# Reordering the sixteen stick-breaking units of a two-block transformer kernel so that the widest unit of a head pair is worked one place later

## The chip, the cores and the metric

The kernel runs on one core of a Trainium2 chip. The metric is the device time of one execution in microseconds (us), lower being better. TensorE (PE in the profile; PEld is its weight load), VectorE (DVE), ScalarE (ACT) and GpSimd (POOL) each work through their own list of instructions in order and wait for each other by semaphores. SyncE (SP) issues most DMAs.

## The reference, cut to what matters

The model has three transformer layers on 512 tokens of width 1024. The first layer has two attentions side by side: eight heads of chunked attention ("a") and eight heads of stick-breaking attention ("b"). The change touches the second one only:

```python
def stick_breaking_attention(q, k, v):
    ...
    for blk in range(s // SB_BLOCK):
        q_start = blk * SB_BLOCK
        k_end = q_start + SB_BLOCK
        logits = jnp.einsum("bqhd,bkhd->bhqk", q[:, q_start:k_end],
                            k[:, :k_end]).astype(jnp.float32) * scale
        strict = (q_start + jnp.arange(SB_BLOCK))[:, None] > jnp.arange(k_end)[None, :]
        log_beta = jax.nn.log_sigmoid(logits)
        log_keep = jnp.where(strict, jax.nn.log_sigmoid(-logits), 0.0)
        log_tail = lax.cumsum(log_keep, axis=3, reverse=True) - log_keep
        weights = jnp.where(strict, jnp.exp(log_beta + log_tail), 0.0).astype(v.dtype)
        outs.append(jnp.einsum("bhqk,bkhd->bqhd", weights, v[:, :k_end]))
```

Afterwards both attention outputs are normalized (their mean squares over the features), scaled by gains, joined and multiplied by `w_out`.

## The kernel before

The kernel holds activations with features on the 128 partitions and the 512 tokens along the free dimension. Each large product is made from a high and a low part of both operands, three matrix products for one. The engine programs are written out by hand, each in its own order, with counting semaphores between them.

Eight heads are four **pairs** `p`, and each pair has four **units** `r` of one block of 128 keys each. Unit `r` treats key block `3 - r` against the queries from that block on, so it is `r + 1` blocks of 128 wide; with two heads its tiles are 256, 512, 768 and 1024 elements wide per partition. I call these widths one to four. `sb_unit(u)` (L705) gives pair, row and first query of the unit at place `u` of the order. Before, it is `u // 4, u % 4`, so the widths run 1 2 3 4, 1 2 3 4, 1 2 3 4, 1 2 3 4.

A unit passes these steps:

1. `sb_qk` (L977, matmuls L985 and the mask L988) on PE: scores into one of three pairs of PSUM banks.
2. The clip (L2323) on DVE: the minimum of the scores and 40, into one of two buffers `tmp`.
3. `softplus` (L1510, instructions L1513 and L1515) on ACT: Exp, then Ln, in place.
4. `sb_larger` (L2278, L2287) on DVE: the maximum of scores and softplus, into `sb_pl`, a ring of three.
5. `sb_tail_sum` (L992) on PE: L998 with the triangle for the unit's own block, and L1005 with ones for what lies in the newer key blocks. For `r = 1` L1005 reads the width-one unit's `sb_pl` directly, for `r` of 2 and 3 it reads the sums `sb_sum`, which `sb_add` (L2290, L2302 and L2303 on DVE) makes after `r = 1` and `r = 2`.
6. `sb_weigh` (L1660, L1667) on ACT: Exp of the banks, which gives the weights `sb_w`.
7. `sb_values` (L1009, L1020) on PE, once for each pair after its width-four unit; `sb_save` (L1670) on ACT copies the result out.

The engines run this as a hand-made pipeline. At step `u` DVE does `sb_larger(u - 1)`, the clip of `u`, then `sb_add(u - 1)` if there is one, and then whatever else was placed there. ACT does `sb_weigh(u - 2)`, then Exp and Ln of `u`. PE does `sb_tail_sum(u)`, the values of the last pair when its turn comes, and `sb_qk(u + 2)`:

```python
                sb_tail_sum(u)
...
                if u and u % 4 == 0:
                    sb_values(u // 4 - 1)
                if u + 2 < SB_UNITS:
                    sb_qk(u + 2)
```

Other work sits at fixed steps: half of a memory product at PE's step 1; the first norm's root on ACT at step 8 (`root("oa")`, two activation table loads and a square root) with its reciprocals on DVE at steps 8 to 10 (L2336); its scaling `scale_a` (L2307) and low parts `low_a` (L2312) on DVE at steps 12 and 13; the high parts `high` on ACT at step 12; squares of the saved pairs at 8, 12 and 16. Before PE's step 15 stand six matmuls of `w_out`. After step 15 follow the rest of them, the values of pair 3, the second norm and the `w_out` phase, which waits for it.

Of the kernel before, what the change touches and what calls it, by code (L numbers as in the profile page):

```python
# [15 lines left out]
ALU = mybir.AluOpType  # L16
# [3 lines left out]
P = 128  # L20
SEQ = 512
# [79 lines left out]
def program(nc, a, out):  # L101
    ctx = ExitStack()
    with ctx:
# [16 lines left out]
        act_lo = at("act_lo", [P, KT, SEQ], o_act + 16 * KB, FP32R)  # L120

        sb_pl = at("sb_pl", [P, 3, 2, SEQ], o_act)
        sb_w = at("sb_w", [P, 2, 2, 1280], o_act + 12 * KB)
        sb_sum = at("sb_sum", [P, 2, 2, SEQ], o_m + 80 * KB)
        p_low_0 = at("p_low_0", [P, 2, 768], o_m + 64 * KB)
# [576 lines left out]

        SB_UNITS = 4 * 4

        def sb_unit(u):  # L705

            p, r = u // 4, u % 4
            return p, r, P * (3 - r)

        def sb_banks(u):  # L710

# [39 lines left out]
        def _(pe):  # L751
# [240 lines left out]
            def sb_tail_sum(u):  # L992

                p, r, q0 = sb_unit(u)
                b = [bank[sb_banks(u) + h] for h in range(2)]
                pe.wait_ge(sb_plus, u + 1)
                for h in range(2):
                    last = pe.matmul(b[h][:, q0:SEQ], neg_upper[:, :], sb_pl[:, u % 3, h, q0:SEQ],  # L998
                                     start=False, stop=True, skip_group_check=True)
                if r >= 2:  # L1000
                    pe.wait_ge(sb_added, 2 * p + r - 1)
                if r:
                    for h in range(2):
                        older = sb_pl[:, (u - 1) % 3, h, :] if r == 1 else sb_sum[:, r % 2, h, :]
                        last = pe.matmul(b[h][:, q0 + P:SEQ], neg_ones[:, :], older[:, q0 + P:SEQ],  # L1005
                                         start=False, stop=True, skip_group_check=True)
                last.then_inc(sb_tail, 1)

            def sb_values(p):  # L1009
                if p == 0:  # L1010
                    pe.wait_ge(out_saved, PAIR0["mem_a"])
                if p == 1:
                    pe.wait_ge(root_ready, NORM["oa"] + 1)
                if p >= 2:
                    pe.wait_ge(sb_saved, p - 1)
                pe.wait_ge(sb_weights, 4 * p + 4)
                for kj in range(4):
                    for h in range(2):
                        head = 2 * p + h
                        last = pe.matmul(bank[p % 2][HD * h:HD * h + HD, P * kj:SEQ],  # L1020
                                         v_tok[1][:, kj, HD * head:HD * (head + 1)],
                                         sb_weight(p, 3 - kj, h), start=kj == 0, stop=True,
                                         skip_group_check=True)
                last.then_inc(sb_out, 1)
# [136 lines left out]
            for u in range(SB_UNITS):  # L1161
                if u == 15:
                    pe.wait_ge(w_ready, C0["w_out"] + 1)
                    pe.wait_ge(act_ready, SPLIT0["w_out"] + 4)
                    pe.wait_ge(sb_saved, 3)
                    part(C0["w_out"], 0, 0, range(2), o_0, start=True)
                sb_tail_sum(u)
                if u == 1:
                    pe.wait_ge(out_saved, 4)
                    mem_half(1, 1)  # L1170
                if u == 4:
                    pe.wait_ge(mem_saved, 2)
                if u and u % 4 == 0:
                    sb_values(u // 4 - 1)
                if u + 2 < SB_UNITS:
                    sb_qk(u + 2)
                if u == 5:
                    norm_sum("oa")
            part(C0["w_out"], 0, 0, range(2, 4), o_0)
            sb_values(3)  # L1180
# [223 lines left out]
        def _(act):  # L1404
# [273 lines left out]
            for u in range(SB_UNITS + 2):  # L1678
                if u >= 2:
                    sb_weigh(u - 2)  # L1680
                if u < SB_UNITS:
                    softplus(sb_clip(u), sb_clamped, sb_exped, sb_logged, u + 1)
                if u == 0:
                    square("oa", 3, o_raw[0][:, 3, :], (out_saved, 4))
                if u in (5, 9, 13):
                    sb_save(u // 4 - 1)
                if u == 8:
                    root("oa")
                    act.preload_act_table_set("natural_log_exp_and_others")
                if u in (8, 12, 16):  # L1690
                    square_b(u // 4 - 2)
                if u == 12:
                    for t in range(4):
                        high("w_out", t, o_hi_0[0][:, t, :], buf=rel[0])
            sb_save(3)
# [132 lines left out]
        def _(dve):  # L1828
# [449 lines left out]
            def sb_larger(u):  # L2278

                p, r, q0 = sb_unit(u)  # L2280
                b = sb_banks(u)
                dve.wait_ge(sb_logged, u + 1)
                if u == 0:
                    dve.wait_ge(chunk_done, C0["w_out"])
                if u >= 3:
                    dve.wait_ge(sb_tail, u - 1 if r == 3 else u - 2)
                dve.tensor_tensor(sb_pl[:, u % 3, :, q0:SEQ], banks[:, b:b + 2, q0:SEQ], sb_clip(u), ALU.max)\  # L2287
                    .then_inc(sb_plus, 1)

            def sb_add(u):  # L2290

                p, r, q0 = sb_unit(u)
                dve.wait_ge(sb_plus, u + 1)
                if u == 1:
                    dve.wait_ge(out_saved, PAIR0["mem_a"])
                if r == 1:
                    older = sb_pl[:, (u - 1) % 3, :, q0 + P:SEQ]
                else:
                    dve.wait_ge(sb_added, 2 * p + 1)
                    older = sb_sum[:, 0, :, q0 + P:SEQ]  # L2300
                new, dst = sb_pl[:, u % 3, :, :], sb_sum[:, (r + 1) % 2, :, :]
                dve.tensor_copy(dst[:, :, q0:q0 + P], new[:, :, q0:q0 + P])  # L2302
                dve.tensor_tensor(dst[:, :, q0 + P:SEQ], new[:, :, q0 + P:SEQ], older, ALU.add)\  # L2303
                    .then_inc(sb_added, 1)
# [10 lines left out]
            for u in range(SB_UNITS + 1):  # L2315
                if u:
                    sb_larger(u - 1)
                if u < SB_UNITS:
                    if u == 0:
# [2 lines left out]
                    b = sb_banks(u)  # L2322
                    dve.tensor_scalar(sb_clip(u), banks[:, b:b + 2, sb_unit(u)[2]:SEQ], CLAMP, None,  # L2323
                                      ALU.min).then_inc(sb_clamped, 1)
                if u and (u - 1) % 4 in (1, 2):
                    sb_add(u - 1)
                if u == 3:
                    mem_group(1)
                if u == 1:
                    add_squares("oa", 3)  # L2330
                if u in (13, 16):
                    add_squares("ob", 1 + u // 16)
                for n in {8: (0, 1), 9: (2,), 10: (3,)}.get(u, ()):
                    c = P * n
                    dve.wait_ge(root_ready, NORM["oa"] + 1)
                    part = dve.reciprocal(rms[:, c:c + P], rms[:, c:c + P])  # L2336
                    if n == 3:
                        part.then_inc(rms_ready, 1)
                if u == 12:
                    dve.wait_ge(rms_ready, NORM["oa"] + 1)  # L2340
                    for t in range(4):
                        scale_a(t)
                    low_a(0)
                    low_a(1)
                if u == 13:
                    low_a(2)
                    low_a(3)
            add_squares("ob", 3)
# [248 lines left out]
```

## Time and profile before

| | |
|---|---|
| median of 3 runs | 1846.5 us (1846.32 to 1847.78) |
| profiled execution, its own time | 1844.83 us |
| span of the profiled execution | 1843.1 us |
| mean granted TensorE clock | 0.995 |
| PE busy | 1793.1 us (97%), 8628 matmuls |
| DVE busy | 1080.7 us (59%) |
| ACT busy | 723.1 us (39%) |

The span runs from the first to the last instruction; the execution's time is 1.7 us more. Busy time is the union of an engine's instructions, so 97% of PE's span says that it seldom stood still, not that it ran at its peak. The stick-breaking units take from about 227 to 302 us of the span.

### The profile page before, as it was taken

How to read it: one execution, taken by the hardware profiler on the slowest of the kernel's cores; microseconds unless marked ns; L12 is line 12 of the kernel's file. 1: busy time of each engine (PE TensorE's matmuls, PEld its weight loads, DVE VectorE, ACT ScalarE, POOL GpSimd, SP SyncE). 2: the span in 40 equal slices, each digit the busy share in tenths (PEclk: the TensorE clock that was granted, in tenths of full speed). 3: DMA queues.
4: the chain of work that ended last, by engine and by line, in shares of the span. 5: the costliest groups of instructions: out<-in, count | busy, mean ns of one | idle time of the engine just before them, and what ended most of it. 6: DMA issues, size and time to landing. Idle time of an engine off the chain costs nothing.

```text
span 1843.1 us, 23045 instructions
## 1 busy us (share of the span) xinstructions
PE 1793.1 (97%) x8628; PEld 1445.4 (78%) x8628; DVE 1080.7 (59%) x1569; ACT 723.1 (39%) x1015; POOL 38.8 (2%) x78
## 2 busy tenths in 40 slices
PE   6999988999999999999999999999999999999998
PEld 5787645788888888878888888889766788888886
DVE  6576755656655425765767675245467467776423
ACT  4212654343443323443443433233356344444322
POOL 3110000000000000000000000000000000000000
PEclk9999999999999999999999999999999999999999
DMA  9685110423322233322322322323401223322231
GB/s 328 236 320 179 47 52 19 141 80 101 104 91 91 87 102 93 107 70 71 112 91 91 105 100 80 108 81 105 164 24 47 69 92 95 110 91 91 91 103 69
DMA packets 148059, 195.32 MB, mean 106 GB/s; under 512 B 3646, under 2 KB 133000, under 8 KB 144284
## 3 DMA queue, kind: packets, MB, share of 16 engines
q1 hardware_dynamic: 141272, 155.28, 25.9%
q0 software_dynamic: 6576, 39.13, 5.6%
q8 instruction: 43, 0.70, 0.2%
q14 instruction: 20, 0.16, 0.0%
q10 hardware_dynamic: 148, 0.05, 0.0%
HBM read 189.15 MB, written 5.29 MB: 105 GB/s over the span
## 4 chain that ended last, share of the span: by engine, by line
PE 89%; DVE 5%; ACT 3%; DMA 1%; issue 1%; SPq 0%; DVEq 0%; ACTq 0%
PE bank L770 21%; PE bank L771 21%; PE bank L772 21%; PE bank L833 3%; PE bank L835 2%; PE bank L834 2%; PE bank L1385 2%; PE bank L1383 2%; PE bank L1384 2%; PE bank L916 2%; PE bank L952 2%; PE bank L933 1%; PE bank L813 1%; PE bank L814 1%; PE bank L815 1%
## 5 line engine op out<-in xcount | busy, mean ns | idle before, releaser
L1832 DVE TENSOR_TENSOR w_lo<-w_stage,w_hi 128x2048 fp32r<-128x2048 f32 (+2 forms) x137 | 301.3, 2199 | 469.5 <-ACT w_hi L1410 469.3
L770 PE MATMUL bank<-act_hi,w_hi 128*128 128x512 f32 x1232 | 482.9, 392 | 4.8 <-DVE act_lo L2163 3.4
L771 PE MATMUL bank<-act_lo,w_hi 128*128 128x512 f32 x1232 | 480.1, 390 | 0.0
L772 PE MATMUL bank<-act_hi,w_lo 128*128 128x512 f32 x1232 | 480.0, 390 | 0.0
L1410 ACT ACTIVATE w_hi<-w_stage 128x2048 fp32r<-128x2048 f32 (+3 forms) x139 | 255.5, 1838 | 490.5 <-PE bank L772 370.1
L770 PEld LDWEIGHTS bank<-act_hi,w_hi 128*128 128x128 f32 x1232 | 231.7, 188 | 57.4 <-issue 3.3
L772 PEld LDWEIGHTS bank<-act_hi,w_lo 128*128 128x128 f32 x1232 | 231.7, 188 | 48.4
L771 PEld LDWEIGHTS bank<-act_lo,w_hi 128*128 128x128 f32 x1232 | 231.7, 188 | 47.8 <-issue 0.5
L770 PE MATMUL bank<-mid_hi,w_hi 128*128 128x512 f32 x352 | 136.9, 389 | 0.0
L771 PE MATMUL bank<-mid_lo,w_hi 128*128 128x512 f32 x352 | 136.9, 389 | 0.0
L772 PE MATMUL bank<-mid_hi,w_lo 128*128 128x512 f32 x352 | 136.9, 389 | 0.0
L1553 ACT ACTIVATE mid_hi<-tmp 128x512 f32 x66 | 40.7, 633 | 97.1 <-DVE tmp L2036 97.1
L772 PEld LDWEIGHTS bank<-mid_hi,w_lo 128*128 128x128 f32 x352 | 66.1, 188 | 13.8
L770 PEld LDWEIGHTS bank<-mid_hi,w_hi 128*128 128x128 f32 x352 | 66.1, 188 | 13.7
L771 PEld LDWEIGHTS bank<-mid_lo,w_hi 128*128 128x128 f32 x352 | 66.1, 188 | 13.6
L1383 PE MATMUL bank<-w_hi,mid_hi 128*128 128x512 f32 x176 | 68.8, 391 | 0.0
L1385 PE MATMUL bank<-w_lo,mid_hi 128*128 128x512 f32 x176 | 68.5, 389 | 0.0
L1384 PE MATMUL bank<-w_hi,mid_lo 128*128 128x512 f32 x176 | 68.5, 389 | 0.0
L1545 ACT ACTIVATE tmp<-tmp,vec 128x512 f32<-128x512 f32 x44 | 33.5, 809 | 70.0 <-DVE tmp L1850 70.0
L1545 ACT ACTIVATE mid_val<-tmp,vec 128x512 f32 x44 | 33.5, 808 | 69.8 <-DVE tmp L1850 69.8
L1850 DVE SCALAR_TENSOR_TENSOR tmp<-bank,rms 128x512 f32<-128x512 f32 x88 | 56.4, 682 | 0.0
L1982 DVE SCALAR_TENSOR_TENSOR ada_acc<-ada_stage,stats,ada_acc 128x2048 f32<-128x2048 f32 x21 | 48.8, 2347 | 1.5 <-DMA ada_stage<-in_w_ada 1.1
(396 smaller groups left out, 2594.8 us busy)
## 6 DMA issues: line engine op xcount, KB each, us to landing
ada_stage<-in_w_ada POOLq DMA_DIRECT2D x24, 1024.0 KB, 7.8
w_stage<-in_w_up SPq DMA_DIRECT2D x22, 1024.0 KB, 5.0
w_stage<-in_a_ffn_in SPq DMA_DIRECT2D x22, 1024.0 KB, 5.1
w_stage<-in_b_ffn_in SPq DMA_DIRECT2D x22, 1024.0 KB, 5.1
w_stage<-in_w_in SPq DMA_DIRECT2D x12, 1024.0 KB, 5.2
w_stage<-in_b_ffn_out SPq DMA_DIRECT2D x10, 1024.0 KB, 5.1
w_stage<-in_w_down SPq DMA_DIRECT2D x8, 1024.0 KB, 5.0
w_stage<-in_a_ffn_out SPq DMA_DIRECT2D x8, 1024.0 KB, 5.0
```

Source lines behind the costliest of these rows:

```text
L770: pe.matmul(dst, wh, mh, start=start and k == 0, stop=False)
L771: pe.matmul(dst, wh, ml, start=False, stop=False)
L772: last = pe.matmul(dst, wl, mh, start=False, stop=stop and k == nk - 1)
L833: pe.matmul(dst, wh, mh, start=start and k == ks[0], stop=False)
L1383: pe.matmul(dst, mh, hi[:, k, :], start=j == 0 and k == 0, stop=False)
L1384: pe.matmul(dst, ml, hi[:, k, :], start=False, stop=False)
L1385: last = pe.matmul(dst, mh, lo[:, k, :], start=False, stop=j == 5 and k == nk - 1)
L1410: act.activation(w_hi[slot][:, 0:n], w_stage[slot][:, 0:n], ACT.Copy).then_inc(w_hi_done, 1)
L1545: act.activation(conv_tile(f, i, s, m), conv_src(f, s, m)[:, :], ACT.Identity, scale=w2, bias=b).then_inc(tap_started, 1)
L1832: dve.tensor_tensor(w_lo[slot][:, 0:n], w_stage[slot][:, 0:n], w_hi[slot][:, 0:n].bitcast(FP32), ALU.subtract).then_inc(w_ready, 1)
L1850: return dve.scalar_tensor_tensor(out=dst, in0=src[:, :], scalar=scale, in1=norm[:, :], op0=ALU.mult, op1=ALU.mult)
L1982: dve.scalar_tensor_tensor(out=acc, in0=ada_stage[n][:, :], scalar=k, in1=acc, op0=ALU.mult, op1=ALU.add).then_inc(ada_added, 1)
```

## The change

The order of the units is written out in a list. The width-four unit of pairs 0, 1 and 2 changes places with the width-one unit of the next pair, so that the widths run 1 2 3 1 4 2 3 1 4 2 3 1 4 2 3 4. What hangs on places follows: the values of a pair, its save, the first norm's sum and root, the reciprocals, the scaling and the low and high parts come one step later. The width-one unit's softplus gets a buffer of its own, `sb_pl_first`, because its reader (`r = 1`) is now two places behind it. Two waits are added on DVE: `sb_larger` of a width-four unit waits for its pair's second sum, and the second `sb_add` of a later pair waits until the last width-four tail sum has read `sb_sum`. The wait of `sb_larger` on `sb_tail` for width four goes from `u - 1` to `u - 2`. No instruction that computes is added or removed, and no DMA is touched.

```diff
+        sb_pl_first = at("sb_pl_first", [P, 2, SEQ], o_m + 18 * KB)
...
+        SB_ORDER = [(0, 0), (0, 1), (0, 2), (1, 0), (0, 3), (1, 1), (1, 2), (2, 0), (1, 3), (2, 1), (2, 2), (3, 0),
+                    (2, 3), (3, 1), (3, 2), (3, 3)]
+
         def sb_unit(u):
 
-            p, r = u // 4, u % 4
+            p, r = SB_ORDER[u]
             return p, r, P * (3 - r)
+
+        def sb_at(p, r):
+
+            return SB_ORDER.index((p, r))
+
+        def sb_plus_of(u):
+
+            return sb_pl_first[:, :, :] if sb_unit(u)[1] == 0 else sb_pl[:, u % 3, :, :]
...
 # sb_tail_sum
-                    last = pe.matmul(b[h][:, q0:SEQ], neg_upper[:, :], sb_pl[:, u % 3, h, q0:SEQ],
+                    last = pe.matmul(b[h][:, q0:SEQ], neg_upper[:, :], sb_plus_of(u)[:, h, q0:SEQ],
...
-                        older = sb_pl[:, (u - 1) % 3, h, :] if r == 1 else sb_sum[:, r % 2, h, :]
+                        older = sb_pl_first[:, h, :] if r == 1 else sb_sum[:, r % 2, h, :]
...
 # sb_values
-                pe.wait_ge(sb_weights, 4 * p + 4)
+                pe.wait_ge(sb_weights, sb_at(p, 3) + 1)
...
 # PE's loop
-                if u == 4:
+                if u == 5:
                     pe.wait_ge(mem_saved, 2)
-                if u and u % 4 == 0:
+                if u in (5, 9, 13):
                     sb_values(u // 4 - 1)
                 if u + 2 < SB_UNITS:
                     sb_qk(u + 2)
-                if u == 5:
+                if u == 6:
                     norm_sum("oa")
...
 # ACT's loop
-                if u in (5, 9, 13):
+                if u in (6, 10, 14):
                     sb_save(u // 4 - 1)
-                if u == 8:
+                if u == 9:
                     root("oa")
                     act.preload_act_table_set("natural_log_exp_and_others")
-                if u in (8, 12, 16):
+                if u in (9, 13, 16):
                     square_b(u // 4 - 2)
-                if u == 12:
+                if u == 13:
                     for t in range(4):
                         high("w_out", t, o_hi_0[0][:, t, :], buf=rel[0])
...
 # sb_larger
-                    dve.wait_ge(sb_tail, u - 1 if r == 3 else u - 2)
-                dve.tensor_tensor(sb_pl[:, u % 3, :, q0:SEQ], banks[:, b:b + 2, q0:SEQ], sb_clip(u), ALU.max)\
+                    dve.wait_ge(sb_tail, u - 2)
+                if r == 3:
+                    dve.wait_ge(sb_added, 2 * p + 2)
+                dve.tensor_tensor(sb_plus_of(u)[:, :, q0:SEQ], banks[:, b:b + 2, q0:SEQ], sb_clip(u), ALU.max)\
                     .then_inc(sb_plus, 1)
...
 # sb_add
                 if r == 1:
-                    older = sb_pl[:, (u - 1) % 3, :, q0 + P:SEQ]
+                    older = sb_pl_first[:, :, q0 + P:SEQ]
                 else:
                     dve.wait_ge(sb_added, 2 * p + 1)
+                    if p:
+                        dve.wait_ge(sb_tail, sb_at(p - 1, 3) + 1)
                     older = sb_sum[:, 0, :, q0 + P:SEQ]
...
 # DVE's loop
-                if u and (u - 1) % 4 in (1, 2):
+                if u and sb_unit(u - 1)[1] in (1, 2):
                     sb_add(u - 1)
...
-                if u in (13, 16):
+                if u in (14, 16):
                     add_squares("ob", 1 + u // 16)
-                for n in {8: (0, 1), 9: (2,), 10: (3,)}.get(u, ()):
+                for n in {9: (0, 1), 10: (2,), 11: (3,)}.get(u, ()):
...
-                if u == 12:
+                if u == 13:
                     dve.wait_ge(rms_ready, NORM["oa"] + 1)
                     for t in range(4):
                         scale_a(t)
                     low_a(0)
                     low_a(1)
-                if u == 13:
+                if u == 14:
                     low_a(2)
                     low_a(3)
```

## Rows read from the trace of the kernel before

**Rows 1.** The page's chain of waits, shares of the span by engine.

```profile
PE 89%; DVE 5%; ACT 3%; DMA 1%; issue 1%; SPq 0%; DVEq 0%; ACTq 0%
```

**Rows 2.** One window, a pair long: stretch, length, busy times, granted clock, DMA.

```profile
262.50:280.50 18.00, 13.97 (x68) 7.56 (x68) 11.02 (x17) 12.63 (x17) 0.00 (x0) 1.00 0.00 0
```

**Rows 3.** Waits between 226 and 302 us: total, times, longest.

```profile
DVE tmp L2323 <- PE bank L988: 11.0, 5, 4.2
```

**Rows 4.** Timeline of DVE: start, duration, instruction, idle time before it.

```profile
239.92 1.22 DVE L2323 TENSOR_SCALAR tmp<-bank 128x1024 f32<-128x1024 f32 x1 [2.79 <-PE bank L988]
...
244.49 0.41 DVE L2323 TENSOR_SCALAR tmp<-bank 128x256 f32<-128x256 f32 x1
...
245.84 0.42 DVE L2287 TENSOR_TENSOR sb_pl<-bank,tmp 128x256 f32<-128x256 f32 x1 [0.93 <-ACT tmp L1515]
...
250.49 0.69 DVE L2323 TENSOR_SCALAR tmp<-bank 128x512 f32<-128x512 f32 x1 [4.23 <-PE bank L988]
...
252.54 0.69 DVE L2287 TENSOR_TENSOR sb_pl<-bank,tmp 128x512 f32<-128x512 f32 x1 [1.36 <-ACT tmp L1515]
...
289.28 0.96 DVE L2323 TENSOR_SCALAR tmp<-bank 128x768 f32<-128x768 f32 x1 [1.17 <-PE bank L988]
...
292.03 0.96 DVE L2287 TENSOR_TENSOR sb_pl<-bank,tmp 128x768 f32<-128x768 f32 x1 [1.25 <-ACT tmp L1515]
292.90 1.21 DVE L2323 TENSOR_SCALAR tmp<-bank 128x1024 f32<-128x1024 f32 x1
...
296.33 1.22 DVE L2287 TENSOR_TENSOR sb_pl<-bank,tmp 128x1024 f32<-128x1024 f32 x1 [1.42 <-ACT tmp L1515]
```

**Rows 5.** Timeline of PE in pair 3, at the full clock.

```profile
280.65 1.98 PE L998 MATMUL bank<-sb_pl,neg_upper 128*128 128x512 f32 x4 [1.51 <-DVE sb_pl L2287]
...
283.85 0.70 PE L985 MATMUL bank<-qkv 64*128 64x256 f32 x4
...
285.17 0.71 PE L998 MATMUL bank<-sb_pl,neg_upper 128*128 128x128 f32 x4 [0.40 <-DVE sb_pl L2287]
285.81 2.37 PE L1020 MATMUL bank<-sb_w,vb_tok 128*64 128x512 f32 x16
288.11 0.92 PE L985 MATMUL bank<-qkv 64*128 64x384 f32 x4
...
289.08 1.08 PE L998 MATMUL bank<-sb_pl,neg_upper 128*128 128x256 f32 x4
...
290.54 1.13 PE L985 MATMUL bank<-qkv 64*128 64x512 f32 x4
...
293.04 1.56 PE L998 MATMUL bank<-sb_pl,neg_upper 128*128 128x384 f32 x4 [1.15 <-DVE sb_pl L2287]
```

**Rows 6.** Timeline of PE in pair 0, from where the orders part.

```profile
238.53 1.13 PE L985 MATMUL bank<-qkv 64*128 64x512 f32 x4
...
239.72 1.51 PE L998 MATMUL bank<-sb_pl,neg_upper 128*128 128x384 f32 x4
...
242.02 0.49 PE L985 MATMUL bank<-qkv 64*128 64x128 f32 x4
...
244.63 3.26 PE L998 MATMUL bank<-sb_pl,neg_upper 128*128 128x512 f32 x4 [1.91 <-DVE sb_pl L2287]
...
249.53 0.70 PE L985 MATMUL bank<-qkv 64*128 64x256 f32 x4
```

**Rows 7.** One window of the slow stretch, columns as in Rows 2.

```profile
246.00:247.00 1.00, 1.00 (x3) 0.48 (x2) 0.26 (x1) 0.00 (x0) 0.00 (x0) 0.50 0.42 168
```

**Rows 8.** Timeline of DVE: the first norm's extra work.

```profile
265.89 1.76 DVE L2336 RECIPROCAL rms<-rms 128x128 f32<-128x128 f32 x2 [2.93 <-ACT rms L1440]
267.57 0.36 DVE L2287 TENSOR_TENSOR sb_pl<-bank,tmp 128x256 f32<-128x256 f32 x1
...
280.84 2.73 DVE L2307 SCALAR_TENSOR_TENSOR rel<-oa_raw,vec,rms 128x512 f32<-128x512 f32 x4
...
284.69 0.42 DVE L2287 TENSOR_TENSOR sb_pl<-bank,tmp 128x256 f32<-128x256 f32 x1
```

More of the change, by code:

```diff
@@ L2296, in sb_add @@
                 if r == 1:
-                    older = sb_pl[:, (u - 1) % 3, :, q0 + P:SEQ]
+                    older = sb_pl_first[:, :, q0 + P:SEQ]
                 else:
                     dve.wait_ge(sb_added, 2 * p + 1)
+                    if p:
+                        dve.wait_ge(sb_tail, sb_at(p - 1, 3) + 1)
                     older = sb_sum[:, 0, :, q0 + P:SEQ]
-                new, dst = sb_pl[:, u % 3, :, :], sb_sum[:, (r + 1) % 2, :, :]
+                new, dst = sb_plus_of(u), sb_sum[:, (r + 1) % 2, :, :]
                 dve.tensor_copy(dst[:, :, q0:q0 + P], new[:, :, q0:q0 + P])
```

## The prediction, made before the changed kernel was run

> **What bounds the kernel now.** I read four views. The chain of waits first: PE carries 89% of it, DVE and ACT together 8% [rows 1], so nearly all of the kernel is a row of matmuls and a gain can only lie where PE is not the chain. The unit stage is such a place. In the window of one pair, PE is busy 13.97 of 18.00 us and DVE and ACT no more, 11.02 and 12.63 [rows 2]: no engine is full, the chain crosses from one to the other. The waits say where: the clip waits five times for the scores, 11.0 us in all [rows 3]. The timeline then gives each step its price, and I lay out the new order with them.
>
> **The prices.** DVE and ACT form one loop: clip, Exp, Ln, larger, and the next clip starts 0.08 us before the larger ends. From a clip to its larger it takes 1.35, 2.05, 2.75 and 3.43 us for widths one to four, and from there to the next clip the larger's own 0.42, 0.69, 0.96 or 1.22 less 0.08 [rows 4]. So the loop alone needs 1.69, 2.66, 3.63 and 4.57 us a unit, 12.5 for four.
>
> PE starts a tail sum 0.06 us after its larger ends: 0.48 after its start for width one (284.69 to 285.17), 1.01 for three (292.03 to 293.04), so 0.75 and 1.28 for two and four [rows 4, 5, 8]. A tail sum holds PE 0.64, 1.46, 2.30 and 3.20 us (285.17 to 285.81, 289.08 to 290.54, 239.72 to 242.02, 280.65 to 283.85), values 2.30, and scores 0.97 for width three and 1.19 for four, that is 0.21 less a width, so 0.76 and 0.56 for two and one [rows 5, 6]. A clip can start 0.2 us after the scores have let PE go: 1.39 after their start for width four (238.53 to 239.92), 1.17 for three, 0.96 for two, hence 0.74 for one [rows 4, 5, 6]. PE's work for four units comes to 7.60 + 3.48 + 2.30 = 13.4 us.
>
> The hole lies here: the scores of unit u + 2 stand behind the tail of u. Before, the width-four tail (1.28 + 3.20) and the scores behind it take 5.4 us from the larger to the clip, while the loop beside it has a width-one unit, 2.8 us.
>
> **The change, part by part.** It adds and removes no computing instruction and no DMA; SP's and POOL's queues are passed by nothing. What moves is the order. Laid out from 238.53, where both orders part (times of the new order, PE at its full clock; the row's 238.53 stands, since the matmuls of the memory half before it stay) [rows 6]:
>
> *Places 3 to 7.* Scores 3 (width one) start at 238.53, tail 2 at 239.09, scores 4 (width four) at 241.39, so clip 4 starts at 242.78 and larger 4 at 246.21. Tail 3 and scores 5 are over at 243.93; PE then has nothing until tail 4 at 247.49. That is an idle stretch of 3.56 us where before it was 1.91 [rows 6]. Tail 4 ends at 250.69, and scores 6 open clip 6 at 251.86, where DVE was free at 250.00. Larger 6 starts at 254.61. Tail 5, the values of pair 0 and scores 7 follow each other on PE from 251.66 to 255.98; clip 7 starts at 256.16, tail 6 at 255.98, scores 8 at 258.28, clip 8 at 259.67.
>
> *Places 8 to 11.* Larger 8 is at 263.10, clip 9 at 264.24, tail 8 from 264.38 to 267.58. ACT's root now comes after Ln of unit 9. Before, the reciprocals waited 2.93 us after the clip had ended [rows 8], and of this Exp and Ln of width one were 0.9, so the root costs 2.03. Ln 9 ends at 266.25, the reciprocals start at 268.28, hold DVE 1.68 (265.89 to 267.57) [rows 8], and larger 9 starts at 269.96 instead of 266.29. The stall of 3.7 us is the one that was there before, with another unit under it. Clip 10 follows at 270.56, larger 10 at 273.31; tail 9, the values and scores 11 keep PE from 270.70 to 275.02, tail 10 to 277.32, so clip 11 is at 275.20 and clip 12, behind scores 12, at 278.71. The other two reciprocals lie beside Exp and Ln; the norm's sum lies in PE's idle time before tail 8 (2.7 us); without that cover it would put its 0.9 us on the loop.
>
> *Places 12 to 15.* Larger 12 is at 282.14, tail 12 from 283.42 to 286.62, clip 13 at 283.28. Scaling and two low parts took DVE from 280.84 to 284.69, 3.85 us [rows 8]; now they run from 283.88, and larger 13 comes at 287.73 instead of 285.33. Tail 13 starts at 288.47, then values 2, then scores 15 at 292.23: clip 15 at 293.62, larger 15 at 297.05. Before, larger 15 started at 296.33 [rows 4]. The other low parts and the squares delay larger 14 by about 0.5 us, under clip 15's wait for PE. The added waits, on sums and tails which are over by then, cost nothing: what stands behind them on DVE, the larger of width four and the second add, has its input later than they are met. If such a wait were met late, DVE's clip and then ACT's Exp would be late by as much. The saves and weights on ACT come out at least 0.5 us before PE asks for them.
>
> So at the full clock the new order is **0.7 us slower** than the row. The same hole stands twice in a pair now, each smaller: the wide scores wait behind the width-three tail with a width-one unit as cover (clips 4, 8 and 12), and those of width three behind the wide tail (clip 6; at clip 10 the root hides it). In exchange, before, pair 0 had lost more than the pattern.
>
> **The clock.** In 246 to 247 us the granted clock is 0.50, 1.2 GHz, after PE had stood idle for 1.91 us [rows 6, 7]. The wide tail then takes 4.90 us (244.63 to 249.53) instead of 3.20, a loss of 1.7, and clip 5 waits 4.23 [rows 4, 6]. That loss is in the row of 296.33. In the new order PE idles for 3.56 us in the same place, before the same wide tail. I take it that the clock falls again: 1.7 us more, and nothing hides it, since clip 6 waits for that tail. The sum is 0.72 + 1.70 = **2.4 us**. The idle stretches before tails 8 and 12, 2.7 and 3.6 us, may bring it too, but there tail 9 waits for the root (2.1 us of room) and tail 13 for the scaling (0.9 us of room), so at most 0.8 us would come through. The bounds of the clock's part are thus 0 and 2.5 us.
>
> The Trainium skill (TensorE: Matmul & The Clock Gate, Part 1, "What's actually happening") says that the array falls to half its clock when it has been idle and comes back after sustained work, and that the point shifts from run to run. By that rule all three long idle stretches would be followed by half clock, which by the rooms above would make 3.2 us instead of 2.4. The trace agrees on the two levels, 1.00 and 0.50.
>
> After larger 15 both orders do the same, and the `w_out` phase waits for the second norm, so the shift stays to the end. The profiled execution took 1844.83 us and would take 1847.2; the median of the runs shown lies 1.7 above the profiled one, and I carry the shift to it: 1846.5 + 2.4 = **1848.9 us**.
>
> **The rivals.** *No fall of the clock* (0.22): 0.7 us more, 1847.2. For it: the tails at 280.65 and 293.04 follow idle times of 1.5 and 1.15 us with no sign of it [rows 5]; against it: the new stretch is twice the one that brought it. *A faster kernel* (0.08): PE turns the wide tails and scores out early enough that the clips don't wait for them. It decides if the waits of clips 4, 6, 7, 8, 11, 12 and 15 for PE, in my layout 1.4, 1.9, 0.7, 1.8, 1.0, 1.1 and 1.2 us, all but vanish, 9.1 us together; half of them gone gives 0.7 - 4.6, 1842.6. Against it stand PE's prices, which are read at the full clock. *Clock at half after every long idle stretch, without the rooms* (0.15): 0.7 + 3 x 1.7 = 5.8 us more, 1852.3. It decides when the slow stretch reaches values and scores as well as the tail. The likeliest case has 0.55.
>
> **How the numbers follow.** A measurement of this kernel tells about 0.2%, 3.7 us, from no change. The likeliest case and the first rival lie within it, 0.77, less a little for prices that I carried over 13 places with perhaps 0.1 us of error each: 0.76 within, 0.16 slower, 0.08 faster. The range runs from 1845.0 (first rival less 2.2) to 1851.8 (towards the last rival) and leaves out the faster one.
>
> **What would show it right or wrong.** In the profile after, PE should be idle for about 3.6 us before the first wide tail (L998, 512 columns, about 247.5) and the clock at 0.5 behind it; clip 15 near 295.3 and larger 15 near 298.7 us; the reciprocals' stall of about 3.7 us before larger 9. The prediction is wrong if the clips' waits for PE go well under 11 us in total, or if a fall of the clock lasts beyond one tail.

## The result and the profile after

The changed kernel took 1849.84 us (median of 13 runs, 1848.39 to 1853.91) and the kernel before 1847.68 us (13 runs, 1846.23 to 1850.22). The ratio is 1.0018, with a 95% interval of 1.0011 to 1.0025: some 3.3 us slower, between 2.0 and 4.6; the two medians lie 2.2 us apart. The forecast shift was 2.4 us. The forecast time was 1848.9, 0.9 below the measured one, which lies in the range (1845.0 to 1851.8); the median of before had been taken as 1846.5, from three runs.

The profiled execution took 1849.67 us, span 1848.0, which is 4.9 more than the span before. To find where they came in, I take two marks: the first clip, and the start of the larger of place 15. From here on "clip 11", "larger 11" and "tail 11" are the starts of these steps for the unit at place 11 of the order, and the "stage" runs from clip 0 to larger 15. VectorE's timeline after:

```profile
228.82 0.42 DVE L2339 TENSOR_SCALAR tmp<-bank 128x256 f32<-128x256 f32 x1
...
244.59 1.23 DVE L2339 TENSOR_SCALAR tmp<-bank 128x1024 f32<-128x1024 f32 x1 [1.26 <-PE bank L1000]
248.03 1.22 DVE L2301 TENSOR_TENSOR sb_pl<-bank,tmp 128x1024 f32<-128x1024 f32 x1 [2.21 <-ACT tmp L1527]
...
255.31 0.96 DVE L2339 TENSOR_SCALAR tmp<-bank 128x768 f32<-128x768 f32 x1 [3.41 <-PE bank L1000]
...
267.68 0.68 DVE L2339 TENSOR_SCALAR tmp<-bank 128x512 f32<-128x512 f32 x1
271.71 1.76 DVE L2352 RECIPROCAL rms<-rms 128x128 f32<-128x128 f32 x2 [3.36 <-ACT rms L1452]
273.39 0.63 DVE L2301 TENSOR_TENSOR sb_pl<-bank,tmp 128x512 f32<-128x512 f32 x1
...
287.29 2.73 DVE L2323 SCALAR_TENSOR_TENSOR rel<-oa_raw,vec,rms 128x512 f32<-128x512 f32 x4
289.94 1.29 DVE L2328 TENSOR_TENSOR o_lo<-rel,o_hi 128x512 fp32r<-128x512 f32 x2
291.14 0.69 DVE L2301 TENSOR_TENSOR sb_pl<-bank,tmp 128x512 f32<-128x512 f32 x1
...
301.23 1.22 DVE L2301 TENSOR_TENSOR sb_pl<-bank,tmp 128x1024 f32<-128x1024 f32 x1 [1.42 <-ACT tmp L1527]
```

The larger of place 15 starts at 301.23 against 296.33 [rows 4], 4.9 later; so all of the span's difference is there by then, and the work behind it takes the same time in both. The first clip starts at 228.82. In the trace of before it starts at 227.00:

```profile
227.00 0.42 DVE L2323 TENSOR_SCALAR tmp<-bank 128x256 f32<-128x256 f32 x1
```

So 1.82 us lie ahead of the stage, among instructions that the change does not touch, and **3.08 us in the stage**: 72.41 us from the first clip to that larger, against 69.33. The part ahead varies by itself: in the fourteen profiles of this study the first clip starts between 227.00 and 230.25. In this execution TensorE ran below its full clock there (0.66 over 210 to 220 us, second window below; 1.00 in the trace of before).

TensorE's timeline after, around the first and the last of the three wide tails that moved:

```profile
244.99 0.70 PE L997 MATMUL bank<-qkv 64*128 64x256 f32 x4
245.62 0.29 PE L1000 MATMUL bank<-strict_neg,ident_b 128*128 128x128 bf16 x2
249.31 3.61 PE L1010 MATMUL bank<-sb_pl,neg_upper 128*128 128x512 f32 x4 [3.40 <-DVE sb_pl L2301]
252.75 1.46 PE L1017 MATMUL bank<-sb_sum,neg_ones 128*128 128x384 f32 x4
254.13 0.92 PE L997 MATMUL bank<-qkv 64*128 64x384 f32 x4
...
267.81 1.98 PE L1010 MATMUL bank<-sb_pl,neg_upper 128*128 128x512 f32 x4 [2.54 <-DVE sb_pl L2301]
...
286.83 3.62 PE L1010 MATMUL bank<-sb_pl,neg_upper 128*128 128x512 f32 x4 [3.40 <-DVE sb_pl L2301]
290.28 1.45 PE L1017 MATMUL bank<-sb_sum,neg_ones 128*128 128x384 f32 x4
291.67 0.92 PE L997 MATMUL bank<-qkv 64*128 64x384 f32 x4
```

Windows after (columns as in [rows 2]), and the waits between 226 and 305 us:

```profile
210.00:220.00 10.00, 8.71 (x50) 5.20 (x50) 8.33 (x32) 6.39 (x20) 0.00 (x0) 0.66 0.20 66
250.00:251.00 1.00, 1.00 (x2) 0.34 (x1) 0.00 (x0) 0.97 (x2) 0.00 (x0) 0.50 0.00 0
288.00:289.00 1.00, 1.00 (x3) 0.48 (x2) 1.00 (x3) 0.97 (x3) 0.00 (x0) 0.50 0.00 0
```

```profile
PE bank L1010 <- DVE sb_pl L2301: 13.2, 6, 3.4
DVE tmp L2339 <- PE bank L1000: 13.1, 9, 3.4
```

TensorE stands idle for 3.40, 2.54 and 3.40 us before the three wide tails, where it was 1.91 before the first of them in the old order [rows 6]. The clock is at half behind the first and the third, and each of these tails takes 4.8 us instead of 3.2 (249.31 to 254.13, 286.83 to 291.67), while the second has 1.98 for its 512 columns as at full clock. The clips wait for scores nine times, 13.1 us, where it was five times and 11.0 [rows 3].

### The profile page after: what moved, and what is told of

It is laid out like the page before. It is cut to its first block, busy times and chain, and to the rows that moved or that the text cites. A ratio compares the mean times of both kernels' runs of the same rounds, so it can differ in the third digit from the quotient of the medians.

```text
span 1848.0 us, 23045 instructions
## 1 busy us (share of the span) xinstructions
PE 1797.4 (97%) x8628; PEld 1448.9 (78%) x8628; DVE 1080.9 (58%) x1569; ACT 723.8 (39%) x1015; POOL 38.9 (2%) x78
## 4 chain that ended last, share of the span: by engine, by line
PE 90%; DVE 4%; ACT 3%; DMA 2%; issue 1%; POOL 0%; DVEq 0%; ACTq 0%
PE bank L782 21%; PE bank L783 21%; PE bank L784 20%; PE bank L845 3%; PE bank L847 2%; PE bank L846 2%; PE bank L1397 2%; PE bank L1395 2%; PE bank L1396 2%; PE bank L928 2%; PE bank L964 2%; PE bank L945 1%; PE bank L825 1%; PE bank L826 1%; PE bank L827 1%; DMA ada_stage<-in_w_ada 1%
## 5 line engine op out<-in xcount | busy, mean ns | idle before, releaser
L1395 PE MATMUL bank<-w_hi,mid_hi 128*128 128x512 f32 x176 | 68.9, 392 | 0.0
```

The source lines that it names most:

```text
L1395: pe.matmul(dst, mh, hi[:, k, :], start=j == 0 and k == 0, stop=False)
```

## The experiments

The runs of one kernel differ by up to 0.4% here (1844.3 to 1851.2 us in 29 runs of before), so each kernel is read twice: by its ratio to the kernel before, and by the stage, which the trace of one execution gives to 0.1 us. "Falls" counts the stretches at half clock inside the stage in that execution. "Layout" is the stage as laid out by hand at full clock, in the prediction or in the expectation of the run.

| kernel | ratio (95%) | stage | falls | layout |
|---|---|---|---|---|
| before | | 69.33 | 1 | |
| changed | 1.0018 (1.0011 to 1.0025) | 72.41 | 2 | 70.05 |
| old order in new code | 0.9993 (0.9984 to 1.0002) | 67.62 | 0 | |
| before, filled | 0.9995 (0.9986 to 1.0004) | 67.63 | 0 | |
| changed, three fills | 1.0011 (1.0002 to 1.0020) | 71.70 | 1 | 70.05 |
| changed, four fills | 1.0010 (1.0001 to 1.0020) | 70.09 | 0 | 70.05 |
| first exchange alone | 1.0013 (1.0004 to 1.0022) | 69.63 | 1 | 68.15 |
| middle exchange alone | 1.0014 (1.0004 to 1.0023) | 70.32 | 1, long | 69.6 |
| last exchange alone | 1.0014 (1.0005 to 1.0023) | 73.68 | 3 | 69.4 |
| changed, scaling at step 12 | 1.0019 (1.0010 to 1.0028) | 72.42 | 2 | 69.5 |
| before, values late | 0.9997 (0.9988 to 1.0006) | 68.56 | 1 | |
| before, values and saves late | 0.9986 (0.9977 to 0.9995) | 67.86 | 2 | 64.6 |
| changed, values and saves late | 1.0020 (1.0011 to 1.0030) | 73.30 | 3, one of them long | 68.9 |
| values and saves late, filled | 0.9974 (0.9963 to 0.9985) | 65.08 | 0 | 64.6 to 64.9 |

**Old order in the new code.** Only the list of units and the steps of the other work are put back; the new buffer and the new waits stay.

```diff
-        SB_ORDER = [(0, 0), (0, 1), (0, 2), (1, 0), (0, 3), (1, 1), ...
+        SB_ORDER = [(0, 0), (0, 1), (0, 2), (0, 3), (1, 0), (1, 1), ...
```

> The changed kernel's code (its own buffer for the width-one unit, its waits on the sums) with the old order of units and all other work at its old step. If the order and what follows from it make the difference: no change against before, within 0.4 us. If the buffer's place or the two added waits cost something: up to the 3 us that the change costs.

No cost is seen: the ratio's interval ends at 1.0002, and the stage takes 67.62 us. It came without a fall, and so it is the measure of the old order at full clock; before, with one fall, took 1.71 more. The kernel before with its idle stretch filled (next experiment) has 67.63 without a fall, in the old code. Buffer and waits are not the cause.

**Filling the idle stretches.** Extra matmuls, which nothing reads, keep TensorE busy. In the changed kernel they stand before tails 4, 8 and 12, as below; in the old order there are two, before tail 3:

```diff
+            def fill(n, done):
+                pe.wait_ge(*done)
+                for _ in range(n):
+                    pe.matmul(bank[0][:, :], qkv[:, 16, 0:P], qkv[:, 12, :], start=True, stop=True)
...
+                if u == 4:
+                    fill(3, (mem_saved, 2))
+                if u == 8:
+                    fill(2, (sb_saved, 1))
+                if u == 12:
+                    fill(3, (sb_saved, 1))
                 sb_tail_sum(u)
```

> The new order with eight extra matmuls of 512 columns into a free bank, whose result nothing reads: three before the tail sum of place 4, two before that of place 8, three before that of place 12, each where TensorE was idle. The theory that the order costs 0.7 us and each fall of the clock that nothing covers the rest: no half clock at these three places, the first larger of place 15 starts 0.7 us later than before counted from the scores of place 3, and the time is 0.5 to 1.0 us above the kernel before (some 1.0004). The rival that the order alone makes the whole difference and the clock's fall is covered: the time stays about 3 us above before (1.0018), clock or no clock. The rival that the extra matmuls run past the idle time: later than the changed kernel.

> The old order with two extra matmuls of 512 columns into a free bank, whose result nothing reads, in the idle 1.9 us before the first wide tail sum. The theory that a fall of the clock costs 1.7 us there: the wide tail and its ones take 3.2 instead of 4.9 us and the kernel is 1.5 us faster than before (0.9991). The rival that the fall is covered by other work: no change. The rival that the fall comes anyway or moves to the next idle stretch: no change, with the half clock at another place of the unit stage.

In the profiles of both, no wide tail ran at half clock. This is TensorE's timeline of the changed kernel with three fills; the idle time is 0.77 us and the tail is short:

```profile
245.54 2.79 PE L1177 MATMUL bank<-qkv 128*128 128x512 f32 x6
249.10 1.98 PE L1010 MATMUL bank<-sb_pl,neg_upper 128*128 128x512 f32 x4 [0.77 <-DVE sb_pl L2313]
```

The clip behind it comes 24.86 us after the first clip, against 26.49 in the changed kernel: 1.63 us gained, near the 1.7 at which the prediction priced the fall. But the clock fell at the one long idle stretch that I had left open, before the tail of place 9, which waits for the root:

```profile
272.25 1.43 PE L1010 MATMUL bank<-sb_pl,neg_upper 128*128 128x256 f32 x4 [1.92 <-DVE sb_pl L2313]
...
274.46 3.30 PE L1032 MATMUL bank<-sb_w,vb_tok 128*64 128x512 f32 x16
```

The values take 3.30 us instead of 2.37, and clip 11 is at 49.82 from the first clip, as late as in the changed kernel (49.81). So the expectation of 0.5 to 1.0 us above the kernel before missed: the ratio says 2.0 us slower, and the stage is 71.70 us.

In the old order the fill gives a stage of 67.63 us, as expected. Its ratio does not decide: the interval, 0.9986 to 1.0004, holds the expected 0.9991 and no change alike. Each run comes with its mean granted clock, and the eleven of this kernel have 0.9936 on average against 0.9927 in the 33 runs of before on the same chip. The fall in the profile of before (granted clock 0.60, 0.50, 0.50 and 0.70 in the four microseconds from 245) is 1.70 of 1843, just such 0.0009. This fits with a fall that is gone from most executions; it does not show it, since falls outside the stage count too. In the new order the fourth fill closes the stretch:

> The new order with extra matmuls of 512 columns into a free bank, nothing reads them, in all four long idle stretches: three before the tail sum of place 4, two before place 8, two before place 9, three before place 12. The earlier fill left out place 9, and the clock fell there. The theory: no fall of the clock in the stage, and 70.05 us from the first clip to the larger of place 15, 2.4 more than the old order's 67.62 without a fall. The rival that the order costs nothing at an even clock: 67.6. The time against before then depends on how often before has its own fall: 0.7 to 2.4 us above it.

The stage takes **70.09 us with no fall; the layout by hand said 70.05**. The ratio, 1.0010, stands against executions of before which have falls of their own. VectorE's first clip and last larger in this kernel, and then in the old order in the new code:

```profile
227.08 0.42 DVE L2353 TENSOR_SCALAR tmp<-bank 128x256 f32<-128x256 f32 x1
...
297.17 1.22 DVE L2315 TENSOR_TENSOR sb_pl<-bank,tmp 128x1024 f32<-128x1024 f32 x1 [1.42 <-ACT tmp L1541]
```

```profile
228.42 0.42 DVE L2339 TENSOR_SCALAR tmp<-bank 128x256 f32<-128x256 f32 x1
...
296.04 1.23 DVE L2301 TENSOR_TENSOR sb_pl<-bank,tmp 128x1024 f32<-128x1024 f32 x1 [1.42 <-ACT tmp L1527]
```

At equal clock the new order costs 70.09 - 67.62 = 2.5 us.

**One exchange at a time.** The list of units holds only one of the three exchanges, and the other work stands at the step that goes with it, for the last one for instance:

```diff
+        SB_ORDER = [(0, 0), (0, 1), (0, 2), (0, 3), (1, 0), (1, 1), (1, 2), (1, 3), (2, 0), (2, 1), (2, 2), (3, 0),
+                    (2, 3), (3, 1), (3, 2), (3, 3)]
```

> Only the first exchange is made (width four of pair 0 with width one of pair 1); pairs 1 to 3 keep the old order and their other work its old step. Counted from the first clip to the larger of place 15, a stretch that took 67.62 us in the old order when the clock did not fall. The theory that the exchanges each cost what the layout by TensorE's order of work gives: 68.15 us, or 0.5 more, plus 1.6 to 1.7 for a fall of the clock before the first wide tail sum. The rival that each exchange costs the same third of the 2.4 us: 68.4. The rival that the exchange itself is free and only the clock costs: 67.6 or, with one fall, 69.3.

> Only the last exchange is made (width four of pair 2 with width one of pair 3), with the scaling, high and low parts one step later as in the change; pairs 0 to 2 keep the old order. From the first clip to the larger of place 15, the layout gives 69.4 us at the full clock, 1.8 more than the 67.62 of the old order, since clip 12 waits 2.1 us for the wide scores, and clip 15 for scores that stand behind the scaling, the tail and the values. With a fall of the clock before the tail of place 12 some 0.8 more, with one in pair 0 another 1.7. The rival that the exchanges cost a third each: 68.4. The rival that only the clock costs: 67.6 without a fall.

> Only the middle exchange is made (width four of pair 1 with width one of pair 2), the root and its reciprocals one step later as in the change; pairs 0 and 3 as in the old order. The layout gives 69.6 us from the first clip to the larger of place 15 at the full clock, 2.0 more than 67.62, because the values of pair 1 now stand ahead of the wide scores of pair 2, which in the full change stand a place later; with a fall of the clock in pair 0 another 1.7. So the costs of the exchanges would not add up: 0.4 + 2.0 + 1.8 alone, 2.4 together. The rival that they add up leaves 0.2 for this one: 67.9, or 69.5 with one fall.

The first: 69.63 us with one fall on the wide tail. It costs a little less than in the changed kernel, since its start lies in idle time (granted clock 0.74 over 249 to 250 us, the tail starts at 249.90):

```profile
249.90 3.45 PE L1010 MATMUL bank<-sb_pl,neg_upper 128*128 128x512 f32 x4 [3.40 <-DVE sb_pl L2301]
...
254.57 0.92 PE L997 MATMUL bank<-qkv 64*128 64x384 f32 x4
```

That is 4.67 us instead of 3.20, and clip 6 stands at 26.32 from the first clip against 24.87 in the kernel with four fills, whose order is the same up to there. Less these 1.45 the stage is 68.18, against 68.15 laid out.

The middle: larger 9 comes 5.72 us after its clip (37.74 to 43.46), as laid out in the prediction (264.24 to 269.96). The fall lies on the wide tail of place 8, which with its ones takes 5.93 us instead of 3.20 (266.36 to 272.29). The root covers most of this; clip 10 waits 0.89 us for TensorE, and the stage is 0.7 over its layout, 70.32 against 69.6.

The last has three falls, and its timeline of TensorE shows the second and third:

```profile
276.60 2.50 PE L1010 MATMUL bank<-sb_pl,neg_upper 128*128 128x384 f32 x4 [1.79 <-DVE sb_pl L2301]
278.90 1.81 PE L1017 MATMUL bank<-sb_sum,neg_ones 128*128 128x256 f32 x4
280.64 1.13 PE L997 MATMUL bank<-qkv 64*128 64x512 f32 x4
...
286.74 3.26 PE L1010 MATMUL bank<-sb_pl,neg_upper 128*128 128x512 f32 x4 [3.40 <-DVE sb_pl L2301]
```

The first fall makes clip 11 come 1.70 late (48.95 from the first clip, against 47.25 in the old order at full clock). Worked on from there with the prediction's prices, the second makes clip 12 a further 1.74 late (54.52 against 52.78) and the third clip 15 a further 0.80 (70.24 against 69.44); 69.4 plus these is 73.6, measured 73.68.

So at full clock each exchange costs something alone: 0.6 us for the first (68.18 less 67.62), and 2.0 and 1.8 by the layout for the others. No profile has these two without a fall, but both come out right once their falls are put in. Together the three cost 2.5 and not 4.4. They don't add up; by the layout this is because the values stand ahead of another unit's scores in each, which no run tests by itself.

**The scaling back at step 12.**

```diff
-                if u == 13:
+                if u == 12:
                     dve.wait_ge(rms_ready, NORM["oa"] + 1)
                     for t in range(4):
                         scale_a(t)
+                if u == 13:
                     low_a(0)
```

and on ACT the four high parts at step 12.

> The changed kernel with the four scalings back at VectorE's step 12 and the four high parts back at ScalarE's step 12, so that they lie beside the width-four unit; the low parts stay at steps 13 and 14. If the scaling at step 13 is what holds up larger 13: larger 13 comes 1.5 to 2.0 us earlier. On what follows the two theories part: if TensorE's order of work bounds this pair, the tail of place 13 still stands behind the wide tail and the scores of place 14, and the larger of place 15 comes only 0.5 us earlier, 69.5 us at the full clock plus what falls of the clock add (some 1.6 in pair 0, up to 1.7 before place 12, where there is no room now). If the scaling is the bound, the whole 2 us come through.

Larger 13 comes 60.17 us after the first clip instead of 62.32, so the scaling did hold it up. The end of the stage does not move, 72.42 against 72.41: clip 14, at 64.03 and 64.02, waits for scores behind the wide tail, which ran at half clock in both. With that fall TensorE's row of work is the bound there. Whether 0.5 us would come at full clock, no profile shows.

**Values behind the scores.** In the trace of before, clips 6, 10 and 14 (width three) wait 1.13, 1.72 and 1.17 us for their scores, and the values stand ahead of these on TensorE.

```diff
-                if u and u % 4 == 0:
-                    sb_values(u // 4 - 1)
                 if u + 2 < SB_UNITS:
                     sb_qk(u + 2)
+                if u and u % 4 == 0:
+                    sb_values(u // 4 - 1)
```

> The old order with the values of pairs 0 to 2 put behind the scores of their step on TensorE instead of ahead of them. If the clips of width three wait because 2.3 us of values stand ahead of their scores, as the timeline of before shows (waits of 1.1, 1.7 and 1.2 us), each pair gets about 1.0 us shorter and the kernel is 3 us faster than before (0.9983); if the wait only moves to the next tail sum, no change.

It gave 0.8 us in the stage instead of 3, and a ratio that is not clear of 1. ScalarE's timeline says where the gain went:

```profile
253.73 0.63 ACT L1515 ACTIVATE tmp<-tmp 128x512 f32<-128x512 f32 x1
256.22 0.60 ACT L1673 ACTIVATE ob_raw<-bank 128x512 f32<-128x512 f32 x1 [1.86 <-PE bank L1020]
256.71 0.38 ACT L1667 ACTIVATE sb_w<-bank 128x256 f32<-128x256 f32 x1
256.97 0.84 ACT L1513 ACTIVATE tmp<-tmp 128x768 f32<-128x768 f32 x1
```

The save (L1673) now waits 1.86 us for the later values, and the next Exp (L1513) stands behind it. The saves are moved one step later, to take that wait away:

```diff
-                if u in (5, 9, 13):
+                if u in (6, 10, 14):
                     sb_save(u // 4 - 1)
```

> The old order, with the values of pairs 0 to 2 behind the scores of their step and the save of each pair on ScalarE one step later, so that the save no longer holds up the next Exp. If the gain of the values' move was lost to that save: from the first clip to the larger of place 15 it takes 64.6 us at the full clock, 3.0 less than the old order's 67.62, and the kernel is 3 us faster than before (0.9984). If it was lost on TensorE, where the next tail sum stands behind the values: 66.8, as with the values alone.

Clip 7 then comes 30.14 us after the first clip instead of 30.75, and 30.98 in the kernel before. The stage takes 67.86 us with two falls, one more than in the profile of before, and the ratio is 0.9986, clear of 1. The 64.6 us were for full clock, and are tested below. The same two moves in the new order:

> The same two moves in the new order (values of pairs 0 to 2 behind the scores of their step, saves one step later). By the layout the first two pairs gain nothing, because in the new order the wide scores wait behind the width-three tail sum and not behind the values, and pair 2 gains 1.2 us: 68.9 us from the first clip to the larger of place 15 at the full clock against 70.05, plus 1.6 to 1.7 for a fall before the first wide tail sum and up to 0.8 for one before that of place 12. The rival that the values are the wait in the new order too: 67.0, 3.0 less.

73.30 us with three falls, ratio 1.0020. Clip 11, of width one, comes 1.1 us sooner after larger 8 than in the kernel with four fills (11.0 against 12.1 us), but clip 12, of width four, does not (15.7 against 15.6), as expected: its scores stand behind the width-three tail, not behind the values. The first fall lasted through tail, values and scores here and made larger 8 come 3.2 us late (39.28 from the first clip, 36.11 with four fills), so what pair 2 may have gained is lost, and the kernel is no faster than the changed one. Its layout of 68.9 us at full clock was not tested.

**Both together in the old order.**

> The old order with the values behind the scores and the saves one step later, and with extra matmuls of 512 columns that nothing reads in TensorE's idle stretches: two before the tail of place 3, one before 7 and one before 8, two before 11. The theory that both gains stand side by side: no fall of the clock, 64.6 to 64.9 us from the first clip to the larger of place 15 against 67.62 for the old order at the full clock, and 4 us faster than before (0.9978). The rival that the extra matmuls delay the tails behind them: 66 us or more.

65.08 us without a fall, and 1843.83 us against 1847.53 us (medians; ratio 0.9974, interval 0.9963 to 0.9985): some 4.8 us faster than the kernel before, the lowest ratio of all, though its interval overlaps that of the same kernel without fills. By the medians alone it is 3.7 us. The fill does not delay what stands behind it: the first wide tail starts at 246.44, 1.28 us after its larger, as it does without a fill:

```profile
244.47 1.98 PE L1165 MATMUL bank<-qkv 128*128 128x512 f32 x4
246.44 1.98 PE L998 MATMUL bank<-sb_pl,neg_upper 128*128 128x512 f32 x4
```

The stage is 0.2 us over what was expected, and why was not tried. What of the gain over before comes from the order of work and what from the fills is only told apart in the stage, whose profiles differ by 4.25 us: 2.5 by the order of work (65.08 against 67.62 at full clock) and 1.7 by the fall that did not come. Of the 2.5, the values alone give 0.8: the kernel with values late has 68.56 us, less 1.69 for its fall (clip 5 at 23.49 against 21.80) 66.87. The saves' move gives the other 1.8.

## Why the prediction was right

**The layout.** The step-by-step layout at full clock gave 70.05 us from the first clip to the larger of place 15 (297.05 less 227.00) and 70.09 was measured with the clock held up. The stall of the reciprocals was forecast at 3.7 us; larger 9 came 3.66 after it could have (273.39 less 267.68 and the 2.05 of a width-two unit). The idle stretches were forecast at 3.56, 2.7 and 3.6 and came out as 3.40, 2.54 and 3.40, each some 0.2 shorter; I take it that this is because the profile counts idle time from the end of the last matmul and I had counted from when TensorE could start the next.

**The clock.** It fell after the idle stretch before the first wide tail, as I took it to, and cost 1.6. The prediction gave the two others "at most 0.8" together and left them out of the sum. One of them did come, before the tail of place 12; from the layout with the first fall (71.7) to the 72.41 measured it is 0.7. That makes the 3.08 us of the profiled execution out of 2.4, and it is the term that was mis-sized: the likeliest case should have held a fall at every idle stretch of more than 3 us, with its room. The profiles of this study bear that out. In the stage, all nine idle stretches of 3.4 us or more (3.40 to 3.75) were followed by half clock; of the three of 2.54 us, one; of the twelve of 1.8 to 1.9 us, seven; after shorter ones the clock never fell.

The Trainium skill (TensorE: Matmul & The Clock Gate, Part 1, "What's actually happening") says that an idle TensorE goes to half its clock. I had read it as a fall after each of the three long stretches, which made 3.2 us; that is nearer to 3.08. The reading went beyond the page, which does not say that every such stretch is enough, and the trace has two falls of the three. The 2.54 us before the second wide tail brought none in this execution. In the new order with values and saves late they did, and the root hid it: larger 9 comes 5.72 us after its clip there, as elsewhere.

**How the sum was put.** "At the full clock 0.7 us slower than the row" set an order without a fall against a row that held one. At equal clock it is 2.4, measured 2.5, and the falls of both orders come on top. The sum was the same, but said like this it hides that most of the cost is the order of work: without any fall of the clock the new order is still slower. In the profiles the 3.08 us are these 2.5, plus 2.3 for the two falls of the new order (72.41 less 70.09), less 1.7 for the one of the old.

**Where luck came in.** The shift was read from one profiled execution of before, with one fall in the stage and less half clock ahead of it than in most other profiles, and carried to medians of executions that have other falls. The mean granted clock of the changed kernel's runs is 0.991, that of before 0.9927 to 0.9929 in its 29 to 33 runs on each of three chips. The one fall more in the stage explains about half of this difference; where the rest lies, no run shows. So the stage is accounted for to 0.1 us, while the agreement of 2.4 with the 2.2 to 3.3 us of the whole kernel is in part luck.

**The rivals.** *No fall of the clock* did not come: there were two. Nor are the falls the whole cost: 70.09 without one is still 2.5 over 67.62. *A faster kernel* did not come: the clips' waits for TensorE grew to 13.1 us, and were 10.8 in the kernel with four fills, against 9.3 in the old order at full clock. *Clock at half after every long idle stretch, without the rooms* did not come in the profile of the changed kernel, but the new order with values and saves late shows that one fall can cost 3.2 us.

## What to carry to other kernels

Moving a wide unit away from a narrow one does not close a hole if the engine that is late works its list in order: here the hole was TensorE's tail and scores in a row, and the exchange opened it in a second place of some pairs. What narrowed it in the old order (clips waiting 6.8 us instead of 9.3 at full clock) was to put work that nobody waits for yet (the values) behind work that somebody waits for (the scores), and to move its reader as well. When a stage is a relay between engines, count what an idle TensorE does to its own clock, for idle time is not free even where no work is lost in it.

## What was not expected of the hardware

The same code gives executions that differ by where TensorE's clock falls. In the kernel before, the clock fell in the stage in one profile; in the same order under the new code it did not, after an idle stretch of 1.91 and 1.90 us. In the unchanged part ahead of the stage it fell in the trace of after and not in that of before, worth 1.8 us. Behind the stage, seven of the fourteen profiles have a fall near 1,410 us (0.83 over 1410 to 1420 us in the kernel before with values late, 1.00 in that of before), and in them the span from larger 15 to the end is 1548.1 us or more, against 1546.7 to 1546.9 in the others.

The timed runs agree with this: of 29 runs of the kernel before on one chip, the seven with a mean granted clock of 0.994 have a median of 1844.6 us, the twelve with 0.993 1847.0, and the seven with 0.992 1848.1. The changed kernel's thirteen lie at 0.991 on average, their times from 1848.4 at 0.993 to 1852.1 at 0.989 (median of three). So at 0.992, 1848.1 us before (seven runs) stand against 1849.4 after (five), though these come from different sets of runs. The clock's falls go with most of the spread of 4 us or more between runs of one kernel, and so a stage's length with its falls counted told more here than a median.

Work that fills idle time, of no use in itself, paid in the stage: 1.63 us at one place. Whether it pays in the median by itself is not shown.
